# Gate projections of a recurrence in pieces of two to five products between the links of its chain

## The chip, the cores and the metric
The kernel runs on one core of a Trainium2 chip. The metric is the device time of one execution in microseconds (us). All arithmetic is in 32-bit floats. The engines named below are PE (TensorE: its matmuls, and PEld for its weight loads), DVE (VectorE), ACT (ScalarE), POOL (GpSimd) and SP (SyncE, which issues the DMAs).

## The reference, cut to what matters
Two transformer blocks are computed over 256 tokens of width 1024. The second block has two branches from one projection: sparse attention and an RWKV-7 recurrence. Both are gated and merged, and a mixture of 32 experts follows.

```python
xn = _rmsnorm(h, mix_norm_g[l]) * (1.0 + sc1) + sh1
proj = xn @ w_in[l]
q_a, kv_lat, q_i, k_i, w_i, p_shift, gate_a, gate_r = _split(proj, IN_SPLITS)
...
def step(state, inp):
    r_t, d_t, k_t, v_t, kk_t, b_t = inp
    sa = jnp.einsum('bhij,bhj->bhi', state, -kk_t)
    state = state * d_t[:, :, None, :] + sa[..., None] * b_t[:, :, None, :] + v_t[..., None] * k_t[:, :, None, :]
    y = jnp.einsum('bhij,bhj->bhi', state, r_t)
    return state, y
...
merged = jax.nn.sigmoid(gate_a) * (o_attn @ w_branch_attn[l]) + jax.nn.sigmoid(gate_r) * (o_rwkv @ w_branch_rwkv[l])
```

The change touches `gate_a` and `gate_r` (the gate projections: 256 tokens, 1024 in, 2048 out) and the stage in which they are computed, which is the one that turns the token-by-token recurrence into matrices over chunks.

## The kernel before, in words
The recurrence has 8 heads of width 64 and 256 tokens. The stage at L2474 to L2709 makes, for each head and each half of the tokens (16 units `u`), the matrices of the chunked form. This needs the inverse of a triangular 128x128 matrix. It is built by a chain of products in which every link depends on the one ahead of it, over PE, ACT and DVE. Two units, `b` = 0 and 1, go side by side as a **pair**; there are eight pairs, in a loop at L2606. Unit `b` works in the PSUM banks `ps[4b]` to `ps[4b + 3]`.

PE's queue is in the order of the program. In one pair the list `steps` (L2543 to L2592) has twelve steps k = 0 to 11, and of each step the first unit's part comes ahead of the second's:

- k = 0, `start_` (L2514): the six products of both units that everything starts from. It waits for `i_end`, that is for ACT's last copy of the pair ahead (`nmap`, L2636).
- k = 1, 2 and 4, `level` (L2549, products at L2554 and L2556): squarings. Their results are copied by ACT (`sq`, L2620).
- k = 3, 5 and 6, `grow` (L2560): products that DVE adds to the growing inverse (`grown`, L2677). Level 1 waits for DVE's `first` (L2665), seven masked products for each unit.
- k = 7, 8 and 9, `off1`, `off2`, `off3` (L2567 to L2581): a transpose, the products outside the diagonal blocks, and a last grow. `off2` also makes two products into `ps[B + 3][:, 0:128]`, which ACT copies (`uh`, L2627).
- k = 10, `solve` (L2583). DVE copies and spreads its results (`sol`, L2692).
- k = 11, `maps` (L2528): the maps of the state for both units. DVE (L2700) and then ACT (`nmap`) take them out.

The gate projections need 32 tiles of 128x128, each the sum of 8 products over chunks of 128 of the inner dimension (`gate_product`, L2593). 8 tiles are computed in the stage ahead and the other 24 here, three in each pair, `GATE_AFTER = (0, 10, 11)` sets them behind the steps 0, 10 and 11, each as one run of eight products. A product over one chunk is two PE instructions in the trace. Their banks are `gate_bank` (L2496): columns 128 to 255 of ps3, ps3 and ps7. ACT turns each tile into gates (`gate_sigmoid`, L2646) at its places k = 0 and k = 5 of a pair and behind the pair. `side_gate` counts finished tiles, `side_gate_out` the sigmoids. SP loads the weights of the two branch projections when the tenth and the eighteenth tile are done (L2489).

The next stage (L2722) runs the chain of states over the chunks, and behind it come the merge, the router and the experts, whose weights are streamed from memory.

Of the kernel before, what the change touches and what calls it, by code (L numbers as in the profile page):

```python
# [19 lines left out]
P = 128  # L20
# [3 lines left out]
KC = D // P  # L24
# [23 lines left out]
def build(nc, inp, out, debug=None, until=99):  # L48
    ctx = ExitStack()
    with ctx:  # L50
# [5 lines left out]
        def sem(name):  # L56
            if name not in sems:
                sems[name] = nc.alloc_semaphore(name)
            return sems[name]
# [58 lines left out]
        ps = [ctx.enter_context(nc.psum_tensor(f"ps{i}", [P, 512], F32)) for i in range(8)]  # L118
# [1569 lines left out]
        with nc.Block() as block:  # L1688
            @block.sync
            def _(sp):  # L1690
                start_sync(sp)
                attention_sync(sp)
                output_sync(sp)
# [45 lines left out]
        LORA, GATE0 = 6, 7  # L1739
# [44 lines left out]
        def p2_ready(pe, i):  # L1784
            pe.wait_ge(sem(f"p2_loaded{i % MIX_CELLS}"), p2_loads[i])
# [688 lines left out]
        with nc.Block() as block:  # L2474
# [3 lines left out]
            def inst(u):  # L2478


                h, t = 2 * (u // 4) + u % 2, u // 2 % NT
                jo = (h % 2) * 64
                return h, t, slice(jo, jo + 64), h // 2, u % 2
# [7 lines left out]
                        sem(f"branch_loaded{i}"), 16)  # L2491


            GATE_AFTER = (0, 10, 11)

            def gate_bank(i):  # L2496
                return ps[(3, 3, 7)[i % 3]][:, P:2 * P]

            @block.gpsimd
            def _(pool):  # L2500
# [11 lines left out]
            @block.tensor  # L2512
            def _(pe):
                def start_(u):  # L2514

                    if u >= 2:
                        pe.wait_ge(sem("i_end"), u)
                    for i in range(3):
                        for w in (u, u + 1):
                            h, t, js, q, b = inst(w)  # L2520
                            T = slice(t * P, (t + 1) * P)
                            left = (bT_, kT_, aT_)[i]
                            last = pe.matmul(ps[4 * b + i][:, 0:(S, S, P)[i]], ch4(left)[js, q, T],
                                             tl[js, 0:2, q, T] if i < 2 else ch4(bT_)[js, q, T], start=True, stop=True)
                            if i == 2:
                                last.then_inc(sem("i_prod"), 1)

                def maps(u):  # L2528

                    pe.wait_ge(sem("i_gh"), u + 2)  # L2530
                    pe.wait_ge(sem("i_spread"), u + 2)
                    for i in range(3):
                        for w in (u, u + 1):
                            h, t, js, q, b = inst(w)
                            hs = slice(h * 64, (h + 1) * 64)
                            left = (mat(b, UH)[:, 64:P], b_tk[:, t, hs], k_tk[:, t, hs])[i]
                            right = (exp_v[b][:, 0:S], exp_g[b], exp_v[b][:, S:2 * S])[i]
                            last = pe.matmul(ps[4 * b + 2][js, min(i, 1) * S:(min(i, 1) + 1) * S], left, right,
                                             start=(i < 2), stop=(i != 1))
                            if i == 2:  # L2540
                                last.then_inc(sem("i_maps"), 1)

                def steps(u):  # L2543

                    h, t, js, q, b = inst(u)
                    B = 4 * b
                    hs = slice(h * 64, (h + 1) * 64)

                    def level(n, Q, QT, last_level):  # L2549
                        def f():  # L2550
                            pe.wait_ge(sem(f"i_q{b}"), 4 * (u // 2) + n)
                            if n == 1:
                                pe.wait_ge(sem(f"i_pt{b}"), 5 * (u // 2) + 1)
                            last = pe.matmul(ps[B][:, 0:P], mat(b, QT), mat(b, Q), start=True, stop=True)  # L2554
                            if not last_level:
                                last = pe.matmul(ps[B][:, P:S], mat(b, Q), mat(b, QT), start=True, stop=True)  # L2556
                            last.then_inc(sem(f"i_sq{b}"), 1)
                        return f

                    def grow(n, Q, PT):  # L2560
                        def f():
                            pe.wait_ge(sem(f"i_q{b}"), 4 * (u // 2) + n)
                            pe.wait_ge(sem(f"i_pt{b}"), 5 * (u // 2) + n - 1)
                            pe.matmul(ps[B + 1][:, 0:P], mat(b, Q), mat(b, PT), start=True, stop=True).then_inc(sem(f"i_gr{b}"), 1)
                        return f

                    def off1():  # L2567
                        pe.wait_ge(sem(f"i_pt{b}"), 5 * (u // 2) + 4)
                        pe.transpose(ps[B + 2][:, 0:P], mat(b, PTB), ident[:, :]).then_inc(sem(f"i_pd{b}"), 1)

                    def off2():
                        pe.wait_ge(sem(f"i_off{b}"), 2 * (u // 2) + 1)
                        pe.matmul(ps[B + 2][:, P:S], mat(b, OTM), mat(b, QA), start=True, stop=True).then_inc(sem(f"i_xt{b}"), 1)

                        pe.wait_ge(sem("side_gate_out"), 2 + 3 * (u // 2) + (1, 0)[b])
                        pe.matmul(ps[B + 3][:, 0:64], AKT[b], v_tk[:, t, hs], start=True, stop=True)
                        pe.matmul(ps[B + 3][:, 64:128], RKT[b], v_tk[:, t, hs], start=True, stop=True).then_inc(sem(f"i_u{b}"), 1)

                    def off3():
                        pe.wait_ge(sem(f"i_off{b}"), 2 * (u // 2) + 2)  # L2580
                        pe.matmul(ps[B + 1][:, 0:P], mat(b, QB), mat(b, PTB), start=True, stop=True).then_inc(sem(f"i_gr{b}"), 1)  # L2581

                    def solve():  # L2583
                        pe.wait_ge(sem(f"i_pt{b}"), 5 * (u // 2) + 5)
                        pe.wait_ge(sem(f"i_ud{b}"), u // 2 + 1)
                        pe.matmul(ps[B][:, 0:64], mat(b, PTA), mat(b, UH)[:, 0:64], start=True, stop=True)
                        pe.matmul(ps[B][:, 64:P], mat(b, PTA), a_tk[:, t, hs], start=True, stop=True)
                        pe.matmul(ps[B + 1][js, 0:P], a_tk[:, t, hs], mat(b, PTA), start=True, stop=True).then_inc(sem("i_sol"), 1)

                    return [lambda: None if u % 2 else start_(u), level(1, QA, QTA, False), level(2, QB, QTB, False),  # L2590
                            grow(2, QB, PTA), level(3, QA, QTA, True), grow(3, QA, PTB), grow(4, QB, PTA), off1, off2, off3,
                            solve, lambda: maps(u - 1) if u % 2 else None]  # L2592
                def gate_product(i):  # L2593
                    m, t = 4 + i // NT, i % NT
                    if i % 8 == 0:
                        p2_ready(pe, GATE0 + m // 4)
                    if i % 3 == 0 and i:
                        pe.wait_ge(sem("side_gate_out"), 2 + i - 1)
                    if i % 3 == 2:
                        pe.wait_ge(sem("i_ud1"), i // 3 + 1)  # L2600
                    for c in range(KC):
                        last = pe.matmul(gate_bank(i), p2(GATE0 + m // 4)[:, c, (m % 4) * P:(m % 4 + 1) * P],  # L2602
                                         hT[:, c, t * P:(t + 1) * P], start=(c == 0), stop=(c == KC - 1))
                    last.then_inc(sem("side_gate"), 1)

                for pair in range(8):  # L2606
                    for k, (fa, fb) in enumerate(zip(steps(2 * pair), steps(2 * pair + 1))):
                        fa()
                        fb()
                        if k in GATE_AFTER:  # L2610
                            gate_product(3 * pair + GATE_AFTER.index(k))


            @block.scalar
            def _(act):
# [30 lines left out]
                def gate_sigmoid(i):  # L2646
                    m, t = 4 + i // NT, i % NT
                    act.wait_ge(sem("side_gate"), 2 + i + 1)
                    act.activation(gates_sb[:, m // 4, m % 4, t, :], gate_bank(i), ACT.Sigmoid).then_inc(sem("side_gate_out"), 1)

                for pair in range(8):
                    for k, (fa, fb) in enumerate(zip(steps(2 * pair), steps(2 * pair + 1))):
                        if k in (0, 5):
                            gate_sigmoid(3 * pair + k // 5)
                        fa()
                        fb()
                    gate_sigmoid(3 * pair + 2)

            @block.vector
            def _(v):  # L2660
# [341 lines left out]
```

## Time and profile before
| | us |
|---|---|
| median of 3 runs | 1460.09 |
| lowest and highest of them | 1457.9, 1460.11 |
| the profiled execution | 1459.41 |
| its span in the profile | 1457.7 |
| the stage of the change, within the span | 693.2 to 851.6 |

| engine | busy us | share of the span |
|---|---|---|
| PE matmul | 1153.3 | 79% |
| PE weight load | 673.6 | 46% |
| VectorE | 507.6 | 35% |
| ScalarE | 266.2 | 18% |
| GpSimd | 43.2 | 3% |

The shares are averages over stages that have different limits. In a chain like the one of this stage an engine can be busy for most of the time because its instructions overlap with their own waits, so what counts is which wait ends last ahead of each link. The start of a weight load shows when PE takes up a product. The times in the rows below are us from the start of the span.

### The profile page before, as it was taken

The page shows a single profiled execution, that of the slowest core. Times are in us where ns is not written, and L with a number is a line of the kernel's source. Part 1 is how long each engine was busy: PE and PEld are TensorE (multiplying, and loading weights), DVE is VectorE, ACT ScalarE, POOL GpSimd, SP SyncE. Part 2 cuts the span into 40 slices and gives each one's busy share as a digit, 9 for nine tenths or more (in the row PEclk, how much of TensorE's full clock was granted, in tenths as well). Part 3 has the DMA queues.
Part 4 walks back from the last instruction along what each step waited for, and adds up shares of the span by engine and source line. Part 5 has one row for each costly group of instructions (what it writes and reads, how often), then busy time and mean ns, then how long its engine had stood idle before and what let it go on. Part 6 is the DMA issues. An engine that isn't in the chain of part 4 may idle for free. (4 is left out here: it accounts for less than half of the span.)

```text
span 1457.7 us, 17019 instructions
## 1 busy us (share of the span) xinstructions
PE 1153.3 (79%) x6655; PEld 673.6 (46%) x6655; DVE 507.6 (35%) x1284; ACT 266.2 (18%) x666; POOL 43.2 (3%) x111
## 2 busy tenths in 40 slices
PE   5999869999999795799899996959657567666656
PEld 2788444443343483567777775634122221221212
DVE  1569442222222466758444444242101011010111
ACT  2223212211121212235222220012010100101000
POOL 0000000000000200000111100000000000000000
PEclk8999879999999798888999996979877887787888
DMA  9777636999999793111111010755999999999995
GB/s 373 278 278 273 250 124 272 403 428 428 427 428 383 243 362 122 58 63 54 59 59 51 9 59 1 293 231 224 422 421 422 422 421 422 422 422 422 422 421 230
DMA packets 75155, 404.68 MB, mean 278 GB/s; under 512 B 14075, under 2 KB 15288, under 8 KB 41308
## 3 DMA queue, kind: packets, MB, share of 16 engines
q1 hardware_dynamic: 75100, 403.95, 68.7%
q8 instruction: 35, 0.57, 0.2%
q14 instruction: 20, 0.16, 0.0%
HBM read 402.88 MB, written 1.05 MB: 277 GB/s over the span
## 5 line engine op out<-in xcount | busy, mean ns | idle before, releaser
L1151 PE MATMUL ps<-ring,hT_sb 128*32 128x512 f32 x768 | 119.2, 778 | 71.5 <-DMA ring<-in_expert_w_gate 41.5
L1513 PE MATMUL ps<-ring,hT_sb 128*64 128x512 f32 x448 | 113.2, 595 | 4.2 <-DMA ring<-in_expert_w_gate 2.4
L1151 PEld LDWEIGHTS ps<-ring,hT_sb 128*32 128x32 f32 x768 | 29.0, 137 | 154.9 <-issue 94.0
L1151 PE MATMUL ps<-side,hT_sb 128*32 128x512 f32 x256 | 41.5, 808 | 36.1 <-DMA side<-in_expert_w_up 18.1
L607 PE MATMUL ps<-hT_sb,ring 128*128 128x256 f32 x256 | 61.9, 392 | 2.7 <-ACT hT_sb L352 2.7
L1163 PE MATMUL ps<-ring,tmp 128*32 128x512 f32 x384 | 49.2, 659 | 18.5 <-DMA ring<-in_expert_w_down 18.5
L1760 PE MATMUL ps<-hT_sb,ring 128*128 128x256 f32 (+1 forms) x240 | 61.5, 417 | 0.1
L1217 ACT ACTIVATE hT_sb<-ps,modc 128x128 f32<-128x128 f32 x72 | 27.1, 457 | 188.8 <-PE ps L1134 188.8
L1513 PEld LDWEIGHTS ps<-ring,hT_sb 128*64 128x64 f32 x448 | 35.3, 137 | 55.9 <-issue 51.8
L1255 DVE TENSOR_TENSOR tmp<-ps,tmp 128x512 f32<-128x512 f32 x8 | 5.5, 692 | 154.4 <-ACT tmp L1225 154.4
L1521 PE MATMUL ps<-ring,tmp 128*64 128x512 f32 x256 | 56.7, 595 | 0.0
L607 PEld LDWEIGHTS ps<-hT_sb,ring 128*128 128x128 f32 x256 | 47.9, 194 | 13.6 <-issue 4.6
L1266 DVE COPY hT_sb<-ps 128x512 f32<-128x512 f32 x8 | 5.5, 692 | 136.3 <-PE ps L1163 136.3
L1760 PEld LDWEIGHTS ps<-hT_sb,ring 128*128 128x128 f32 (+1 forms) x240 | 47.6, 203 | 10.8 <-issue 3.3
L1584 ACT ACTIVATE hT_sb<-ps,modc 128x128 f32<-128x128 f32 x72 | 27.1, 456 | 126.9 <-PE ps L1503 126.9
L2602 PE MATMUL ps<-hT_sb,ring 128*128 128x128 f32 x384 | 49.2, 281 | 0.0
L2602 PEld LDWEIGHTS ps<-hT_sb,ring 128*128 128x128 f32 x384 | 44.7, 191 | 5.4 <-issue 4.4
L1163 PE MATMUL ps<-side,tmp 128*32 128x512 f32 x128 | 25.4, 967 | 20.5 <-DMA side<-in_expert_w_down 20.5
L1151 PEld LDWEIGHTS ps<-side,hT_sb 128*32 128x32 f32 x256 | 9.7, 143 | 67.8 <-issue 25.3
L1261 DVE TENSOR_TENSOR tmp<-ps,tmp 128x512 f32<-128x512 f32 x8 | 5.5, 691 | 89.0 <-PE ps L1151 89.0
L214 DVE SCALAR_TENSOR_TENSOR acc<-side,cond,acc 128x1024 f32<-128x1024 f32 x28 | 35.8, 1280 | 0.8
L1163 PEld LDWEIGHTS ps<-ring,tmp 128*32 128x32 f32 x384 | 12.1, 120 | 49.3 <-issue 26.2
(515 smaller groups left out, 1906.7 us busy)
## 6 DMA issues: line engine op xcount, KB each, us to landing
ring<-in_expert_w_gate SPq DMA_DIRECT2D x12, 4096.0 KB, 34.5
ring<-in_expert_w_up SPq DMA_DIRECT2D x12, 4096.0 KB, 34.8
ring<-in_expert_w_down SPq DMA_DIRECT2D x12, 4096.0 KB, 33.3
ring<-in_expert_w_down SPq DMA_DIRECT2D x16, 2048.0 KB, 15.9
ring<-in_expert_w_up SPq DMA_DIRECT2D x16, 2048.0 KB, 18.3
ring<-in_expert_w_gate SPq DMA_DIRECT2D x12, 2048.0 KB, 19.4
side<-in_ada_w SPq DMA_DIRECT2D x20, 1024.0 KB, 6.4
ring<-in_w_in SPq DMA_DIRECT2D x9, 2048.0 KB, 8.5
```

Of the source, the lines that this page charges most:

```text
L214: ins = v.scalar_tensor_tensor(a, w, s, a, ALU.mult, ALU.add)
L607: last = pe.matmul(ps[6][:, w * S:(w + 1) * S], cell(2 * w + h // 4)[:, c, (h % 4) * P:(h % 4 + 1) * P], hT[:, c, :], start=(c == 0), stop ...
L1151: last = pe.matmul(bank[es, :], xg[:, c, es], w[:, e, c % 4, :], start=(c == 0), stop=(c == KC - 1))
L1163: last = pe.matmul(out_ps[h][es, :], hidT[:, f, es], w[:, e, f % 2, h * 512:(h + 1) * 512], start=(f == 0), stop=(f == FC - 1))
L1217: last = act.activation(xg[:, c, :], (gate_ps, up_ps)[half][:, (c % 4) * P:(c % 4 + 1) * P], ACT.Identity, scale=modc[:, 2 * KC + c:2 * KC ...
L1255: v.tensor_tensor(hid, gate_ps[:, :], hid, ALU.mult).then_inc(sem("q_silu"), 1)
L1261: v.tensor_tensor(hid, up_ps[:, :], hid, ALU.mult).then_inc(sem("q_hid_done"), 1)
L1513: last = pe.matmul(bank[e * SLOTS:(e + 1) * SLOTS, :], xg[:, c, e * SLOTS:(e + 1) * SLOTS], dst(e, j, par)[:, c, :], start=(c == 0), stop= ...
L1521: last = pe.matmul(out_ps[h][e * SLOTS:(e + 1) * SLOTS, :], hidT[:, f, e * SLOTS:(e + 1) * SLOTS], dst(e, 2, 0)[:, f, h * 512:(h + 1) * 51 ...
L1584: last = act.activation(xg[:, c, :], (gate_ps, up_ps)[half][:, (c % 4) * P:(c % 4 + 1) * P], ACT.Identity, scale=modc[:, 2 * KC + c:2 * KC ...
L1760: last = pe.matmul(ps[SHIFT_BANKS[m]][0:n, 0:S], p2(i)[:, c, o:o + n], hT[:, c, :], start=(c == 0), stop=(c == KC - 1))
L2602: last = pe.matmul(gate_bank(i), p2(GATE0 + m // 4)[:, c, (m % 4) * P:(m % 4 + 1) * P], hT[:, c, t * P:(t + 1) * P], start=(c == 0), stop= ...
```

## The change
The list `GATE_STEPS` takes the place of `GATE_AFTER`. For each of the three tiles of a pair it says behind which step which chunks are multiplied. The first tile: chunks 0 and 1 behind step 0, chunks 2 to 4 behind step 1, chunks 5 to 7 behind step 2. The second: 0 to 2 behind step 3, 3 to 5 behind step 4, 6 and 7 behind step 5. The third: 0 to 2 behind step 9, 3 to 7 behind step 10. Nothing stands behind step 11 any more. The number of products, their shapes and their operands are the same.

The banks are now ps3, ps7 and ps3. The waits follow them: the first tile of a pair waits for the last sigmoid of the pair ahead, the second for ACT's copy of the second unit in the pair ahead (`i_ud1`), the third for that of the first unit in this pair (`i_ud0`). `off2` waits for the sigmoid of the tile that shares its unit's bank. ACT takes the three sigmoids at its places 2, 3 and 5, ahead of the third squaring's copy, ahead of `uh`, and ahead of `nmap`.

```diff
--- before.py
+++ after.py
@@ -2491,10 +2491,10 @@
                         sem(f"branch_loaded{i}"), 16)
 
 
-            GATE_AFTER = (0, 10, 11)
+            GATE_STEPS = ({0: (0, 2), 1: (2, 5), 2: (5, 8)}, {3: (0, 3), 4: (3, 6), 5: (6, 8)}, {9: (0, 3), 10: (3, 8)})
 
             def gate_bank(i):
-                return ps[(3, 3, 7)[i % 3]][:, P:2 * P]
+                return ps[(3, 7, 3)[i % 3]][:, P:2 * P]
 
             @block.gpsimd
             def _(pool):
@@ -2572,7 +2572,7 @@
                         pe.wait_ge(sem(f"i_off{b}"), 2 * (u // 2) + 1)
                         pe.matmul(ps[B + 2][:, P:S], mat(b, OTM), mat(b, QA), start=True, stop=True).then_inc(sem(f"i_xt{b}"), 1)
 
-                        pe.wait_ge(sem("side_gate_out"), 2 + 3 * (u // 2) + (1, 0)[b])
+                        pe.wait_ge(sem("side_gate_out"), 2 + 3 * (u // 2) + (1, 2)[b])
                         pe.matmul(ps[B + 3][:, 0:64], AKT[b], v_tk[:, t, hs], start=True, stop=True)
                         pe.matmul(ps[B + 3][:, 64:128], RKT[b], v_tk[:, t, hs], start=True, stop=True).then_inc(sem(f"i_u{b}"), 1)
 
@@ -2590,25 +2590,31 @@
                     return [lambda: None if u % 2 else start_(u), level(1, QA, QTA, False), level(2, QB, QTB, False),
                             grow(2, QB, PTA), level(3, QA, QTA, True), grow(3, QA, PTB), grow(4, QB, PTA), off1, off2, off3,
                             solve, lambda: maps(u - 1) if u % 2 else None]
-                def gate_product(i):
+                def gate_product(i, first, end):
+
                     m, t = 4 + i // NT, i % NT
-                    if i % 8 == 0:
-                        p2_ready(pe, GATE0 + m // 4)
-                    if i % 3 == 0 and i:
-                        pe.wait_ge(sem("side_gate_out"), 2 + i - 1)
-                    if i % 3 == 2:
-                        pe.wait_ge(sem("i_ud1"), i // 3 + 1)
-                    for c in range(KC):
+                    if first == 0:
+                        if i % 8 == 0:
+                            p2_ready(pe, GATE0 + m // 4)
+                        if i % 3 == 0:
+                            pe.wait_ge(sem("side_gate_out"), 2 + i)
+                        elif i % 3 == 1 and i > 1:
+                            pe.wait_ge(sem("i_ud1"), i // 3)
+                        elif i % 3 == 2:
+                            pe.wait_ge(sem("i_ud0"), i // 3 + 1)
+                    for c in range(first, end):
                         last = pe.matmul(gate_bank(i), p2(GATE0 + m // 4)[:, c, (m % 4) * P:(m % 4 + 1) * P],
                                          hT[:, c, t * P:(t + 1) * P], start=(c == 0), stop=(c == KC - 1))
-                    last.then_inc(sem("side_gate"), 1)
+                    if end == KC:
+                        last.then_inc(sem("side_gate"), 1)
 
                 for pair in range(8):
                     for k, (fa, fb) in enumerate(zip(steps(2 * pair), steps(2 * pair + 1))):
                         fa()
                         fb()
-                        if k in GATE_AFTER:
-                            gate_product(3 * pair + GATE_AFTER.index(k))
+                        for i, part in enumerate(GATE_STEPS):
+                            if k in part:
+                                gate_product(3 * pair + i, *part[k])
 
 
             @block.scalar
@@ -2650,11 +2656,10 @@
 
                 for pair in range(8):
                     for k, (fa, fb) in enumerate(zip(steps(2 * pair), steps(2 * pair + 1))):
-                        if k in (0, 5):
-                            gate_sigmoid(3 * pair + k // 5)
+                        if k in (2, 3, 5):
+                            gate_sigmoid(3 * pair + (2, 3, 5).index(k))
                         fa()
                         fb()
-                    gate_sigmoid(3 * pair + 2)
 
             @block.vector
             def _(v):
```

## Rows read from the trace of the kernel before
**Rows 1.** The chain that ended last, in order of time: start us, us, what.
```profile
1406.63 33.74 DMA side<-in_expert_w_down
```
**Rows 2.** Windows of the stage: us, busy us of engines (instructions), PEclk, DMA share, GB/s.
```profile
733.00:753.00 20.00, 18.45 (x138) 15.31 (x138) 9.14 (x34) 5.08 (x18) 2.83 (x7) 1.00 0.14 39
```
**Rows 3.** Timeline ahead of the stage: start us, us, engine, line, operation, tiles, count.
```profile
672.72 14.37 PEld L2345 LDWEIGHTS ps<-hT_sb,ring 128*128 128x128 f32 x128
```
**Rows 4.** Timeline of the third pair, and the start of the fourth.
```profile
732.80 1.16 PEld L2523 LDWEIGHTS ps<-tmp 64*128 64x128 f32 x12
...
734.08 1.86 PEld L2602 LDWEIGHTS ps<-hT_sb,ring 128*128 128x128 f32 x16
...
735.64 0.28 DVE L2675 TENSOR_TENSOR ring<-ps,pos_t 128x128 f32<-128x128 f32 x1
...
736.03 0.30 PEld L2554 LDWEIGHTS ps<-acc 128*128 128x128 f32 x2
...
737.68 0.30 PEld L2554 LDWEIGHTS ps<-acc 128*128 128x128 f32 x2 [1.12 <-issue]
...
738.12 0.30 PEld L2554 LDWEIGHTS ps<-acc 128*128 128x128 f32 x2
...
738.86 0.30 PEld L2554 LDWEIGHTS ps<-acc 128*128 128x128 f32 x2 [0.22 <-ACT acc L2624]
...
739.30 0.53 PEld L2564 LDWEIGHTS ps<-acc 128*128 128x128 f32 x4
...
739.75 0.59 PEld L2554 LDWEIGHTS ps<-acc 128*128 128x128 f32 x4
...
740.26 0.60 PEld L2564 LDWEIGHTS ps<-acc 128*128 128x128 f32 x4
...
741.27 0.30 PEld L2564 LDWEIGHTS ps<-acc 128*128 128x128 f32 x2 [0.41 <-issue]
...
744.35 0.53 PEld L2581 LDWEIGHTS ps<-acc 128*128 128x128 f32 x4
...
745.23 0.30 PEld L2586 LDWEIGHTS ps<-acc 128*128 128x128 f32 x2 [0.35 <-DVE acc L2680]
...
747.13 1.86 PEld L2602 LDWEIGHTS ps<-hT_sb,ring 128*128 128x128 f32 x16 [0.17 <-issue]
...
747.64 0.41 DVE L2696 TENSOR_TENSOR ring<-acc,gate_t 128x256 f32<-128x256 f32 x1
749.12 0.20 PEld L2538 LDWEIGHTS ps<-side,acc 128*64 128x64 f32 x4
...
750.56 1.86 PEld L2602 LDWEIGHTS ps<-hT_sb,ring 128*128 128x128 f32 x16 [0.39 <-issue]
...
751.17 0.84 ACT L2639 ACTIVATE ring<-ps 64x256 f32<-64x256 f32 x2 [1.67 <-DVE side L2702]
...
752.54 1.16 PEld L2523 LDWEIGHTS ps<-tmp 64*128 64x128 f32 x12
```
**Rows 5.** Timeline, the last gate product of the stage and its sigmoid.
```profile
849.19 2.05 PE L2602 MATMUL ps<-hT_sb,ring 128*128 128x128 f32 x16
...
851.28 0.28 ACT L2649 ACTIVATE ring<-ps 128x128 f32<-128x128 f32 x1 [0.64 <-PE ps L2602]
```
**Rows 6.** PE in windows (PE busy, PEclk), and two groups of its timeline at either clock.
```profile
646.00:648.00 2.00, 1.11 (x8) 0.87 0.00 0
...
872.00:874.00 2.00, 2.00 (x21) 0.69 0.00 0
874.00:876.00 2.00, 2.00 (x6) 0.50 0.00 0
876.00:878.00 2.00, 2.00 (x11) 0.96 0.00 0
...
866.47 1.99 PE L2736 MATMUL ps<-side,ring 128*128 128x256 f32 x8
...
872.59 3.65 PE L2736 MATMUL ps<-side,ring 128*128 128x256 f32 x8
```

## The prediction
> **What bounds the kernel now.** I read the chain that ended last first: the last 440 us are expert weights on the DMA queues, each load released by a product [rows 1], so whatever ends the work ahead of them later moves the end by as much. The recurrence stage, 693.2 to 851.6 us, lies ahead of it and has almost no DMA. There I read the stage windows: the granted clock is 1.00 (2.4 GHz) and PE is busy 18.4 of 20 us [rows 2]. A busy PE says little here, since links of a chain also wait with matmuls in flight, so I went to the timeline of one pair. The eight pairs repeat each other; the one from 732.80 to the next start at 752.54 has a period of 19.74 us [rows 4]. Times below are counted from its start (S = 732.80), by the starts of weight loads, which show when PE takes up a piece.
>
> In it the three gate products of today cost very different amounts [rows 4]:
> - the one behind the start products runs from 1.28 to 3.23. Level 1 of the first half waits for the seventh mask product on VectorE, which ends at 735.92 (3.12), and starts at 3.23. This gate product is free.
> - the one behind the solve runs from 14.33 to 16.32. What it holds up, the maps, needs the VectorE product that ends at 748.05 (15.25), so about 1.0 us of its 1.99 is exposed.
> - the one behind the maps runs from 17.76 to 19.74. The next start needs the ScalarE copy that ends at 752.01 (19.21), so about 0.5 us is exposed.
> So a pair pays some 1.5 us for its gates, 12 us in eight pairs, out of 47 us of gate work. That is all that any placement can win.
>
> **Where PE really waits.** Between 4.88 (level 1, second half) and grow 4, PE runs level 1, level 2, grow 2, level 3, grow 3 nearly without a gap: 4.88, 5.32, 6.06 (after 0.22 us of idleness), 6.50, 6.95, 7.46 [rows 4]. The larger gaps are the 1.12 us ahead of 4.88, which lies between the two halves of one step, where no piece is put, and 0.41 us ahead of 8.47. This stretch, where 14 of the 24 products go, is already bound by PE.
>
> **The price of a product.** 128 instructions of the same shape back to back have loads over 14.37 us, 0.112 each [rows 3]; a product over one chunk is two of them, 0.224 us. Three are 0.67, two 0.45, eight 1.79; the whole gate behind the solve takes 1.99 until the maps start, 0.20 more, which I give to the change of tile shape.
>
> **The change step by step** (before in brackets, all from [rows 4]):
> 1. Behind the start products two products instead of eight. PE is then idle from 1.73 to 3.23. Level 1 still waits for VectorE: nothing is won, 1.5 us of free cover is given up.
> 2. Behind level 1 (ends 5.32) three products: level 2 of the first half at 5.99 [5.32], second half at 6.43 [6.06, which is when its copy from ScalarE came, so it no longer waits], end 6.88. Three more: grow 2 at 7.55 [6.50].
> 3. Grow 2 takes 0.45, three products: level 3 at 8.67 [6.95]; 0.45 and three more: grow 3 at 9.79 [7.46]; 0.45 and two: PE free at 10.69. Grow 4 came 1.01 behind grow 3, 0.41 of it idle, waiting for VectorE's sum of grow 3's result; that gives 10.80 [8.47]. These last two products are hidden. So of 3.13 us inserted (14 products) 2.33 is on the chain at grow 4, and 0.80 is hidden.
> 4. The transposes and the off-diagonal products keep their distances, 3.08 us to off 3: 13.88 [11.55]. Off 3 takes 0.53, three products 0.67; solve at 15.08, where it came 0.88 behind off 3 [12.43]. Shift 2.65.
> 5. Solve takes 1.90, to 16.98. Five products and the same 0.20: maps at 18.30 [16.32]. VectorE would let them start 2.82 behind solve, at 17.90, so 0.4 us of the old exposure stays. Shift 1.98.
> 6. No gate behind the maps: the next start comes when ScalarE's copy is done, 2.89 behind the maps, and about 0.06 for the semaphore: 21.25 [19.74].
> So a period is 1.51 us longer. In the last pair what follows the maps is the end of the stage: today the last gate's sigmoid ends at 851.56 [rows 5], then it is the copy, which by the same distances (the gate at 849.19, the maps 1.44 ahead of it, the copy's end 2.89 behind them) ends at 850.64, 0.92 us earlier. That pair is 1.98 - 0.92 = 1.06 longer. Sum: 7 x 1.51 + 1.06 = **+11.6 us**. If the 0.20 is not paid by a piece of five and the second halves, which are shifted some 0.15 less at grow 4, decide, it is 1.2 a pair: +9. If each of the eight pieces pays as much as 0.05 (the wait ahead of grow 3 shows 0.06 over four instructions), +0.3 a pair: +14.
>
> **Waits and queues.** ScalarE now takes the first gate's sigmoid ahead of the third squaring copy, the second ahead of the copies of the off-diagonal step, the third ahead of the state map. Each takes 0.28 [rows 5] and each gate is complete at least 1 us before the copy behind it is released (first gate 7.55, level 3's copy 9.2; second 10.69, the off-diagonal copies over 13; third 18.1, the map 20.3), so I cost them at nothing; if one of them were late, it would be 0.28 a pair, 2 us. On PE the new waits of the gates are for copies of the previous pair, or of this pair's first half at off 2, done a whole step earlier. The banks are swapped so that the second gate lies beside the second half's work; off 2 waits for sigmoids that are then long done. SyncE's two branch loads wait for the tenth and the eighteenth gate, and shift by a few us, far ahead of their use. GpSimd's spreads are released by the maps and are done in 3 us of a 20 us period. No DMA moves otherwise.
>
> **The clock.** What the new order does besides is leave PE lean. From the end of the start products (1.28) to level 1 of the second half (4.88) it has 8 instructions of 128 columns in 3.6 us; today there are 20. No stretch of the stage is as lean now, and the clock holds. In the stage ahead, where PE had 8 short instructions in the 2 us from 646, the clock fell to 0.50 (1.2 GHz) [rows 6]. What a fall costs: eight instructions of 256 columns take 1.99 us at the full level and 3.65 at the half one, and the granted clock of the stretches around the latter (0.69, 0.50 and 0.96 over 2 us each) makes some 3.4 us at the half level [rows 6], so 3.4 x (1 - 1.99/3.65) = 1.6 us, all of it on the chain, since behind level 1 PE has no gap left up to grow 4. How many pairs fall the trace doesn't show: bounds none and eight. I take two, nearer to none, because dense work stands on both sides of the lean stretch: +3.2 us (an estimate).
>
> The Trainium skill, TensorE: Matmul & The Clock Gate, section "A second HAM failure mode: psum-queue depth-cycling", says that a PE that idles briefly between groups of matmuls, cycling through banks, has its clock swing between the two levels. By it all eight pairs could fall, which would be the third case below; the trace of before has such short idles in each pair and the clock stays at 1.00, so I give it a small chance.
>
> **Forecast.** The profiled execution took 1459.4 us (its span is 1457.7, 1.7 lies around it); the median of the runs is 0.7 above it. 1459.4 + 11.6 + 3.2 = 1474.2, and with the 0.7 **1474.9 us** for the median.
>
> **Cases.**
> - A, the forecast: the pieces are exposed, and the clock falls in some pairs (one to four): 1471 to 1479. Chance 0.48. For it: the packed stretch and the lean one.
> - B: exposed, and the clock stays: 1460.1 + 11.6 = 1471.7 (1469 to 1474 by the bounds). Chance 0.30. For it: granted 1.00 in all eight pairs today.
> - C: exposed, and the clock falls in five to eight: up to 1460.1 + 11.6 + 12.8 = 1484.5. Chance 0.08.
> - D, the other side: the pieces are hidden. Place: between level 1 and grow 4. The links there are pairs of halves, and each waits for a copy on ScalarE (0.75 to start) or a sum on VectorE; if those waits, not PE, set the pace, the 3.13 us vanish in them. The net of a pair is the shift at grow 4 less 0.82 (0.32 added at solve, 0.67 won to the maps, 0.47 to the start), so it decides at a shift of 0.8, where I find 2.33. With a shift of nothing it is -0.8 a pair, about 7 us, 1453. Against it: the loads of five steps follow each other within 0.06 us but for one gap of 0.22. Chance 0.06.
> - E: the change does nothing to be seen, with the shift near 0.8 (half of the pieces hidden by waits that the starts of loads don't show): 1457 to 1463. Chance 0.08, of which 0.07 is within 0.2% (2.9 us, about what a measurement of this kernel can tell from no change).
> Slower by over 0.2%: A, B, C and the rest of E, 0.87. Faster: D, 0.06. Within: 0.07. The range 1465 to 1483 holds A and B with their bounds and most of C, and leaves out D, E and the top of C, some 0.16.
>
> **What would show it.** In the trace of after: an idle PE of some 1.5 us ahead of level 1 (1.73 to 3.23) in each pair; level 2 starting 1.1 us behind level 1's second half instead of 0.44; grow 4 at 10.8; a period near 21.2 where the clock is 1.00; no PE work between the end of the maps and the next start; in some pairs a granted clock of 0.50 behind the lean stretch. I am wrong if grow 4 comes by 9.3, which makes it D or E; if the period is 21.2 but the stages behind take the difference back; or if the clock is at 1.00 throughout, which makes it B.

## The result and the profile after
The changed kernel takes 1475.5 us (median of 4 runs, 1474.6 to 1477.1), the kernel before 1459.8 (4 runs). The ratio is 1.0115, with a 95% interval of 1.0101 to 1.0129: slower, by 15.7 us. The profiled execution took 1477.1 us, the highest of the four, with a span of 1475.4.

The page of after: busy time of PE, its granted clock in 40 slices, and the end of the chain that ended last.

```profile
PE 1150.9 (78%) x6655; PEld 677.0 (46%) x6655; DVE 507.6 (34%) x1284; ACT 266.1 (18%) x666; POOL 43.2 (3%) x111
...
PEclk8999869999999797889999997888887887887888
...
DMA 25%; PE 6%; DVE 0%; issue 0%; ACT 0%; DVEq 0%; SPq 0%; ACTq 0%
```

PE runs the same 6655 matmul instructions. The end is what it was in [rows 1], expert weights on the DMA queues, only later. The page has nothing that names the change; the stage has.

The eight pairs of after in windows, from one start to the next (the last to the first product of the next stage). Columns: us, PE busy us (instructions), PEclk, DMA share, GB/s.

```profile
693.70:716.59 22.89, 18.86 (x135) 0.93 0.27 92
716.59:737.72 21.13, 17.22 (x134) 1.00 0.00 1
737.72:760.50 22.78, 18.96 (x134) 0.93 0.25 93
760.50:781.63 21.13, 17.22 (x134) 1.00 0.00 1
781.63:802.76 21.13, 17.22 (x134) 1.00 0.00 1
802.76:825.53 22.77, 18.85 (x135) 0.93 0.26 93
825.53:846.66 21.13, 17.22 (x134) 1.00 0.00 1
846.66:868.46 21.80, 17.22 (x134) 1.00 0.01 1
```

A period at full clock is 21.13 us where it was 19.74 [rows 4]. Three pairs have a mean clock of 0.93 and take about 1.65 us more. Before, all eight had 1.00 [rows 2]. The stage, from its first start product to the first product of the next stage, is 174.8 us; it was 159.1 (693.23 to 852.28). The difference is 15.7 us, the whole of what the medians show. The span of the profiled execution is 17.7 us longer: 0.5 of it lies ahead of the stage (which starts at 693.70 and not 693.23), 15.7 in it, and 1.5 behind it, where the next stage took 62.6 us against 59.1 and all that follows it 544.4 against 546.3. The next stage has falls of the clock of its own in both kernels (mean 0.79 before and 0.73 after), and it takes anything from 58.9 to 62.6 us in the profiles of all the runs below, so this difference is not put down to the change.

The fourth pair of after, weight loads only, at full clock. It starts at 760.50; L2606 is now the gate product.

```profile
760.50 1.16 PEld L2523 LDWEIGHTS ps<-tmp 64*128 64x128 f32 x12 [1.89 <-ACT ring L2645]
761.79 0.52 PEld L2606 LDWEIGHTS ps<-hT_sb,ring 128*128 128x128 f32 x4
763.73 0.30 PEld L2554 LDWEIGHTS ps<-acc 128*128 128x128 f32 x2 [1.43 <-issue]
...
765.37 0.30 PEld L2554 LDWEIGHTS ps<-acc 128*128 128x128 f32 x2 [1.12 <-issue]
...
765.81 0.75 PEld L2606 LDWEIGHTS ps<-hT_sb,ring 128*128 128x128 f32 x6
766.48 0.30 PEld L2554 LDWEIGHTS ps<-acc 128*128 128x128 f32 x2
...
768.05 0.53 PEld L2564 LDWEIGHTS ps<-acc 128*128 128x128 f32 x4
768.49 0.75 PEld L2606 LDWEIGHTS ps<-hT_sb,ring 128*128 128x128 f32 x6
769.16 0.53 PEld L2554 LDWEIGHTS ps<-acc 128*128 128x128 f32 x4
...
770.28 0.53 PEld L2564 LDWEIGHTS ps<-acc 128*128 128x128 f32 x4
770.73 0.53 PEld L2606 LDWEIGHTS ps<-hT_sb,ring 128*128 128x128 f32 x4
771.29 0.62 PEld L2564 LDWEIGHTS ps<-acc 128*128 128x128 f32 x4
...
774.35 0.53 PEld L2581 LDWEIGHTS ps<-acc 128*128 128x128 f32 x4
774.79 0.75 PEld L2606 LDWEIGHTS ps<-hT_sb,ring 128*128 128x128 f32 x6
775.47 0.30 PEld L2586 LDWEIGHTS ps<-acc 128*128 128x128 f32 x2
...
777.37 1.19 PEld L2606 LDWEIGHTS ps<-hT_sb,ring 128*128 128x128 f32 x10 [0.17 <-issue]
778.68 0.20 PEld L2538 LDWEIGHTS ps<-side,acc 128*64 128x64 f32 x4
```

Three things to see. PE idles 1.43 us ahead of level 1 (763.73), where the first tile used to be, and again 1.89 ahead of the start products, where the third was. Between 765.37 and 771.29 no row has a bracket, that is, no idle time ahead of it: all pieces but the last lengthen the path, and the last fills the 0.41 us of idleness that stood ahead of grow 4 [rows 4]. And level 1 itself comes no earlier, 3.23 us behind the start as before.

The wait tables of the two kernels fit this, from the side of those who wait for PE. Before, from 693 to 873 us (us in total, times, longest):

```profile
DVE acc L2680 <- PE ps L2564: 24.6, 25, 2.3
...
ACT acc L2624 <- PE ps L2556: 15.7, 24, 1.3
```

After, the same two waits under their new line numbers, of the same stretch:

```profile
ACT acc L2630 <- PE ps L2556: 50.9, 27, 4.0
DVE acc L2685 <- PE ps L2564: 48.1, 25, 5.0
```

ScalarE's wait for a squaring and VectorE's wait for a grow have grown by 35.2 and 23.5 us. They overlap, so they don't add up to the loss, and a part of ScalarE's is only moved: its wait for the gate products fell from 41.4 to 21.6 us, since the sigmoids stand in other places. What the pieces cost is read from the starts above.

### The profile page after: what moved, and what is told of

The parts are those of the page before. It is cut to its first block and busy times, and to the rows that moved or that the text cites. A ratio compares the mean times of both kernels' runs of the same rounds, so it can differ in the third digit from the quotient of the medians.

```text
span 1475.4 us, 17021 instructions
## 1 busy us (share of the span) xinstructions
PE 1150.9 (78%) x6655; PEld 677.0 (46%) x6655; DVE 507.6 (34%) x1284; ACT 266.1 (18%) x666; POOL 43.2 (3%) x111
## 5 line engine op out<-in xcount | busy, mean ns | idle before, releaser
L2606 PE MATMUL ps<-hT_sb,ring 128*128 128x128 f32 x384 | 57.4, 288 | 0.0
L607 PEld LDWEIGHTS ps<-hT_sb,ring 128*128 128x128 f32 x256 | 48.1, 195 | 13.8 <-issue 4.6
L2606 PEld LDWEIGHTS ps<-hT_sb,ring 128*128 128x128 f32 x384 | 50.4, 200 | 2.3 <-issue 1.4
L2685 DVE TENSOR_TENSOR acc<-ps,acc 128x128 f32<-128x128 f32 x64 | 18.7, 292 | 52.3 <-PE ps L2564 48.1
```

The source lines that it names most:

```text
L607: last = pe.matmul(ps[6][:, w * S:(w + 1) * S], cell(2 * w + h // 4)[:, c, (h % 4) * P:(h % 4 + 1) * P], hT[:, c, :], start=(c == 0), stop ...
L2685: v.tensor_tensor(mat(b, dst), ps[B + 1][:, 0:P], mat(b, src), ALU.add).then_inc(sem(f"i_pt{b}"), 1)
```

## The experiments
**Theory 1**, that of the prediction: between level 1 and grow 4 PE itself is the bound, so that products set there are paid; where PE waits, they are free; and the emptied stretches are lean enough (a few instructions between idle times) for the clock to fall. **Theory 2**: the loss is in what came with the pieces, the swapped banks, the new waits and the sigmoids ahead of ScalarE's copies. For the clock the rival is that its falls are not tied to the lean stretches.

Both kernels and all nine runs in one table. The period is that of pairs at full clock, from start to start; "at half" counts pairs in which the clock fell; the stage is measured as above; all three come from one profiled execution of each kernel; the ratio is to the kernel before on the same chip.

| kernel | period | at half | stage | median us | ratio, 95% interval |
|---|---|---|---|---|---|
| before | 19.73 | 0 | 159.1 | 1459.8 | |
| after | 21.13 | 3 | 174.8 | 1475.5 | 1.0115 (1.0101 to 1.0129) |
| first tile whole again | 20.09 | 0 | 161.5 | 1461.8 | 1.0023 (1.0007 to 1.0040) |
| first tile alone in pieces | 20.74 | 2 | 170.4 | 1470.7 | 1.0087 (1.0067 to 1.0108) |
| second tile alone in pieces | 19.99 | 2 | 164.3 | 1465.5 | 1.0056 (1.0037 to 1.0075) |
| the same, gap behind the solve filled | 19.98 | 0 | 161.1 | 1461.9 | 1.0024 (1.0013 to 1.0034) |
| after, gap ahead of level 1 filled | 21.13 | 0 | 169.9 | 1472.0 | 1.0097 (1.0080 to 1.0114) |
| before, four more behind step 3 | 20.54 | 0 | 165.6 | 1467.7 | 1.0063 (1.0047 to 1.0078) |
| before, two more behind step 5 | 19.72 | 0 | 159.0 | 1458.3 | 1.0001 (0.9990 to 1.0011) |
| all where PE waits | 18.26 | 0 | 147.2 | 1446.9 | 0.9924 (0.9910 to 0.9937) |
| the same, none between the halves | 18.86 | 0 | 152.0 | 1451.0 | 0.9947 (0.9932 to 0.9962) |

### One part undone: the first tile whole
```diff
-            GATE_STEPS = ({0: (0, 2), 1: (2, 5), 2: (5, 8)}, {3: (0, 3), 4: (3, 6), 5: (6, 8)}, {9: (0, 3), 10: (3, 8)})
+            GATE_STEPS = ({0: (0, 8)}, {3: (0, 3), 4: (3, 6), 5: (6, 8)}, {9: (0, 3), 10: (3, 8)})
```


> The order of after, but the first tile of each pair again as one run of eight products behind the start products; banks, waits and sigmoids stay those of after. Theory 1 (PE is packed between level 1 and grow 4, and the stretch ahead is lean): only the 6 products that went into the packed stretch come back, so grow 4 comes 1.3 us earlier, a period is 20.1 us, the granted clock is 1.00 in all eight pairs, and the time is 2 to 3 us above before, 1462. Theory 2 (the loss is in the swapped banks, the new waits or the sigmoids ahead of ScalarE's copies): these are all still there, so most of the 15.7 us stays, 1472 to 1475.

Measured: 1461.8, period 20.09, no fall. The one line takes back 13.3 of the 15.7 us of the stage, with banks, waits and sigmoids as in after. So theory 2 can't be the main loss: all that is left for it, together with the pieces of the second and third tile, is 2.4 us.

### One part alone: the first tile in pieces
```diff
-            GATE_AFTER = (0, 10, 11)
+            GATE_STEPS = ({0: (0, 2), 1: (2, 5), 2: (5, 8)}, {10: (0, 8)}, {11: (0, 8)})
...
-                        if k in (0, 5):
-                            gate_sigmoid(3 * pair + k // 5)
+                        if k in (2, 5):
+                            gate_sigmoid(3 * pair + (2, 5).index(k))
```


> The kernel before with its banks and waits; only its first tile is in pieces of 2, 3 and 3 products behind steps 0, 1 and 2, with its sigmoid ahead of the third squaring's copy. Theory 1: six products move from free cover into the packed stretch, at most 1.3 us a pair and about 1.0 by the chain, a period of 20.7 to 21.0 at full clock, and one or more pairs fall to half clock (the stretch behind the start products is as lean as in after), 1.6 us each: 1466 to 1471. Theory 2: without the banks and waits of after the time stays near before, 1460 to 1462.

Measured: 1470.7, period 20.74, falls in the first and the sixth pair. The first tile costs 1.01 us a pair on the kernel before and 1.04 within after (21.13 less 20.09), and it brings the falls with it.

### One part alone: the second tile in pieces
```diff
-            GATE_STEPS = ({0: (0, 2), 1: (2, 5), 2: (5, 8)}, {3: (0, 3), 4: (3, 6), 5: (6, 8)}, {9: (0, 3), 10: (3, 8)})
+            GATE_STEPS = ({0: (0, 8)}, {3: (0, 3), 4: (3, 6), 5: (6, 8)}, {11: (0, 8)})
...
-                        if k in (2, 3, 5):
-                            gate_sigmoid(3 * pair + (2, 3, 5).index(k))
+                        if k in (2, 3):
+                            gate_sigmoid(3 * pair + (2, 3).index(k))
                         fa()
                         fb()
+                    gate_sigmoid(3 * pair + 2)
```


> The order of after for the second tile alone (3, 3 and 2 products behind steps 3, 4 and 5); the first tile is whole behind the start products and the third whole behind the maps. Theory 1: 6 products (1.3 us) go on the chain, 1.0 us exposed behind the solve is won back: period 20.1, 2 to 3 us above before, 1462; if the clock falls, in the gap of 1 us behind the solve that is now empty, 1.6 us more each time. Theory 2 expects nothing here but the cost of the banks, like the first run: over 1470.

Measured: 1465.5 with two falls, and a period of 19.99 at full clock, 0.26 over before. With the first tile whole the third tile in pieces costs 0.10 more (20.09 less 19.99). So a period's 1.40 us divide into 1.04 for the first tile, 0.26 for the second and 0.10 for the third. The 0.26 is net of what the empty place behind the solve wins back, and it would hold any cost of the banks, waits and sigmoids, which are those of after in this run; no run separates these.

The falls sit in another place than those of after. Weight loads of this run around the first of them:

```profile
746.45 0.19 PEld L2588 LDWEIGHTS ps<-acc,side 128*64 128x64 f32 x2
747.79 0.29 PEld L2538 LDWEIGHTS ps<-side,acc 128*64 128x64 f32 x4 [1.15 <-DVE ring L2702]
...
748.70 0.24 PEld L2538 LDWEIGHTS ps<-ring,side 128*64 128x64 f32 x2 [0.19 <-issue]
```

Nothing stands behind the solve here, PE idles 1.15 us, and the maps then run at half clock: their loads are 0.24 us for two, with pauses, and the maps take 2.76 us to the next group (747.79 to 750.55) where they took 1.44 [rows 4].

### That gap filled
Three products of 128x128 are added behind the solve in each pair, into the third tile's bank; nothing uses their results.
```diff
+                def fill(i, n):
+                    pe.wait_ge(sem("i_ud0"), i // 3 + 1)
+                    for c in range(n):
+                        pe.matmul(gate_bank(i), hT[:, c, 0:P], hT[:, c, P:2 * P], start=True, stop=True)
...
+                        if k == 10:
+                            fill(3 * pair + 2, 3)
```


> The run with the second tile alone in pieces, and three idle products behind the solve, where that run's PE stands idle for 0.9 us ahead of the maps and where the clock fell in two pairs just as the maps began (747.8 and 809.2 us). Clock theory: that gap is its second lean place; filled, the clock stays at 1.00, all periods are 20.0 to 20.1, and the kernel is 3 us faster than without the fill, 1462. Rival: the falls come with the time of the execution and not with the gap, and stay: 1465.

Measured: 1461.9. The interval of its ratio lies below that of the run without the fill and just clear of it (1.0034 against 1.0037). The granted clock in the whole stage, first without, then with the fill:

```profile
691.12:855.40 164.28, 144.83 (x1073) 0.98 0.11 39
```
```profile
690.49:851.60 161.11, 148.62 (x1121) 1.00 0.11 40
```
24 products more, which are 48 instructions (1121 against 1073), and the stage is 3.2 us shorter.

### The same in after: the lean stretch filled
Six such products behind the first tile's two, into the second tile's bank.
```diff
+                def fill(i, n):
+                    m = 4 + i // NT
+                    if i > 1:
+                        pe.wait_ge(sem("i_ud1"), i // 3)
+                    for c in range(n):
+                        pe.matmul(gate_bank(i), hT[:, c, 0:P], hT[:, c, P:2 * P], start=True, stop=True)
...
+                        if k == 0:
+                            fill(3 * pair + 1, 6)
```


> The kernel after with six idle products of 128x128 (their results are overwritten) behind the two of the first tile, where PE stands idle for 1.5 us: 48 products more in all, 10.8 us of PE work more. Clock theory: the lean stretch is what lets the clock fall, so it is 1.00 in all eight pairs, every period is 21.1, the three falls of 1.64 us go, and the kernel is 4 to 5 us faster than after with more work: 1470.5. Rival: the falls have nothing to do with that stretch, and they stay (1475), or the products cost their time (1475 and more, period over 22).

Its third pair, weight loads (start at 734.79), and the whole stage in one window:

```profile
736.07 0.52 PEld L2606 LDWEIGHTS ps<-hT_sb,ring 128*128 128x128 f32 x4
736.51 1.42 PEld L2616 LDWEIGHTS ps<-hT_sb 128*128 128x128 f32 x12
738.02 0.30 PEld L2554 LDWEIGHTS ps<-acc 128*128 128x128 f32 x2
```
```profile
692.39:862.27 169.88, 148.09 (x1168) 1.00 0.11 38
```
The twelve added instructions (L2616) take the idle time, level 1 (738.02) comes 3.23 us behind the start as ever, the clock is 1.00 in all eight pairs, and all periods are 21.1. The stage is 4.9 us shorter than in after: the three falls are gone and nothing else is. The median is 3.5 us lower, 1472.0. But the two kernels were measured on different occasions and the intervals of their ratios overlap (from 1.0101 to 1.0114), so that the whole kernel became faster is not shown here; what shows the cause is the clock and the length of the stage. In the pair of runs ahead the ratios show it too.

### The price of a product, in two places
On the kernel before, products of 128x128 with unused results go into ps7: four behind step 3, or two behind step 5.
```diff
+                def fill(i, n):
+                    if i > 2:
+                        pe.wait_ge(sem("side_gate_out"), 2 + i)
+                    for c in range(n):
+                        pe.matmul(ps[7][:, P:2 * P], hT[:, c, 0:P], hT[:, c, P:2 * P], start=True, stop=True)
...
+                        if k == 3:
+                            fill(3 * pair, 4)
```
The other has `if k == 5` and 2 in the last two lines.

> The kernel before with four idle products of 128x128 (0.90 us of PE) behind step 3 in each pair, results unused. Theory 1 (packed): nearly all is on the chain, 0.8 us a pair, period 20.5, 6 to 7 us above before: 1466. Rival (hidden by the waits for ScalarE and VectorE): period 19.7 to 19.9, within 2 us of before.

> The kernel before with two idle products (0.45 us) behind step 5, where grow 4 waits for VectorE, results unused. Theory 1: hidden, period 19.75 and the time within 1 us of before, 1460. Rival (any product between links is paid): 0.45 us a pair, period 20.2, 1463.5.

Measured: four behind step 3 cost 0.81 of their 0.90 us in every period, 6.5 us in the stage (the median is 9.4 above that of before; in its profile the stage also starts 2.0 us later, at 695.2, after work that is the same. That start is anywhere from 690.5 to 695.5 in the profiles of these runs, and is not of the change). Two behind step 5 cost nothing: 19.72, ratio 1.0001. Whether a product is paid is decided by the place and not by being between two links.

### All products where PE waits
In this version tiles run over the end of a pair. In each pair: behind step 0 eight products, between the first and the second half of level 1 four, behind step 5 two, behind step 9 one, behind the solve three, behind the maps six.
```diff
+            GATE_STEPS = {0: ((0, 2, 8), (1, 0, 2)), 5: ((1, 6, 8),), 9: ((2, 0, 1),), 10: ((2, 1, 4),), 11: ((2, 4, 8), (3, 0, 2))}
+            GATE_MID = (1, 2, 6)
...
+                return ps[(7, 3, 3)[i % 3]][:, P:2 * P]
...
                         fa()
+                        if MID and k == 1:
+                            gate_product(3 * pair + GATE_MID[0], *GATE_MID[1:])
                         fb()
```
Each entry is a tile counted from the pair's first, and the chunks from and to. The first tile waits for `i_ud1`, the second for the sigmoids of all tiles up to the last but one, the third for `i_ud0`; the sigmoids are at ScalarE's places 0 and 3 and behind the pair, and `off2` again waits for those of the tiles in its unit's bank.

> All 24 products of a pair where PE waits in the trace: eight behind the start products, four between the two halves of level 1, two behind step 5, one behind step 9, three behind the solve, six behind the maps; tiles run over the end of a pair, banks ps7, ps3, ps3. Theory 1: nothing is exposed but a tenth or two; period 18.4, clock 1.00, the stage 11 us shorter: 1449. Rival (the two halves of a step lose when anything stands between them, since the second half waits behind it): the four in the middle are paid, period 19.2, 1455.

Weight loads of its fourth pair, which starts at 749.38 (L2609 is the gate product here), and the fifth, from 767.64, as a window:

```profile
750.66 1.86 PEld L2609 LDWEIGHTS ps<-hT_sb,ring 128*128 128x128 f32 x16
752.61 0.30 PEld L2557 LDWEIGHTS ps<-acc 128*128 128x128 f32 x2
...
753.05 0.97 PEld L2609 LDWEIGHTS ps<-hT_sb,ring 128*128 128x128 f32 x8
754.25 0.30 PEld L2557 LDWEIGHTS ps<-acc 128*128 128x128 f32 x2 [0.22 <-issue]
...
763.68 0.74 PEld L2609 LDWEIGHTS ps<-hT_sb,ring 128*128 128x128 f32 x6 [0.17 <-issue]
764.66 0.20 PEld L2541 LDWEIGHTS ps<-side,acc 128*64 128x64 f32 x4 [0.23 <-DVE ring L2711]
...
766.11 1.42 PEld L2609 LDWEIGHTS ps<-hT_sb,ring 128*128 128x128 f32 x12 [0.38 <-issue]
767.64 1.17 PEld L2526 LDWEIGHTS ps<-tmp 64*128 64x128 f32 x12
```
```profile
767.64:785.90 18.26, 17.88 (x135) 1.00 0.00 1
```
The second half of level 1 comes 4.87 us behind the start, when it always came, with four products in what was a gap of 1.12. The maps come 0.98 us behind the first load of the gate products that follow the solve, instead of 1.99 [rows 4]. 18.26 is 1.47 less than 19.73, which is the 1.5 us that the prediction found to be all a pair pays for its gates. The stage is 11.9 us shorter, the median 1446.9: faster than both kernels.

> As the run ahead, but the four products stand behind both halves of level 1 and not between them. Theory 1: 0.6 us of their 0.9 are exposed, period 18.9 to 19.0, 5 us above the run ahead: 1454. Rival: no difference between the two.

```diff
-            MID = True
+            MID = False
```
Measured: 1451.0, period 18.86. Behind both halves the same four products cost 0.60 us a pair, 4.8 us in the stage.

## Why the prediction was right
It gave 1474.9; measured were 1475.5. By its own steps, times from a pair's start, the pair at 760.50:

1. Two products behind the start, PE idle, level 1 at 3.23: at 3.23, with 1.43 idle.
2. Level 2 at 5.99, grow 2 at 7.55: 5.98 and 7.55.
3. Level 3 at 8.67, grow 3 at 9.79, grow 4 at 10.80: 8.66, 9.78, 10.79. The last two products are hidden; the run with two more behind step 5 shows the same by itself.
4. Off 3 at 13.88, solve at 15.08: 13.85 and 14.97. This is the one term of the period that was mis-sized. I let off 3 take 0.53, which is how long its loads are in the row; to the next load it is 0.44 (774.35 to 774.79).
5. Maps at 18.30: 18.18, the same 0.1 carried on. The 0.20 was there: ten loads from 777.37 to 778.68 take 1.31, five times 0.224 is 1.12. That it is the change of tile shape was assumed, and no run isolates it.
6. Next start at 21.25: 21.13. 1.40 us a period, not 1.51.

The clock was case A as it was put: three pairs fell, two were taken. Each fall cost 1.64 us (22.78 and 22.77 against 21.13) where 1.6 was worked out from two groups in another stage (3.4 x (1 - 1.99/3.65) is in truth 1.55). One of them, in the pair from 737.72; level 2's loads after the piece are 0.43 apart, where they are 0.22 apart at 766.48:

```profile
743.03 1.03 PEld L2606 LDWEIGHTS ps<-hT_sb,ring 128*128 128x128 f32 x6
743.94 0.55 PEld L2554 LDWEIGHTS ps<-acc 128*128 128x128 f32 x2
744.37 0.55 PEld L2556 LDWEIGHTS ps<-acc 128*128 128x128 f32 x2
```

The sum made again with measured terms: seven periods at 1.40 are 9.8, the last pair 0.96 (21.80 against 20.84), three falls 4.9: 15.7. The prediction had 0.9 us too much for the periods and the last pair and 1.7 too little for the clock, which leaves it 0.9 short; and it started from a median of 1460.1 where the one measured with after is 1459.8. So the miss of 0.6 is small by luck: its parts cancel. The mechanism of the 10.8 us is not luck, since every start was worked out ahead.

The rivals: D and E needed a shift at grow 4 of 0.8 or less; it is 2.32. B would have been 21.1 in all eight pairs. That it is the lean stretches behind which the clock falls was an inference from windows of another stage; the two fills show it, and so does the table: the three orders with such a stretch have 7 falls in 24 pairs, the eight without have none in 64. In the second tile's run the lean stretch lay behind an empty solve. The prediction did not name it, the expectation of that run did; in after the third tile's five products stand there.

How many pairs fall was a guess and stays one. The eight pairs of after are alike on PE and three fell; with the first tile alone it was the first and the sixth, with the second alone the third and the sixth.

The windows of after show something that these pairs have in common: all three have a DMA share of 0.25 to 0.27, and the five others at most 0.01. Are the transfers the cause? Finer windows of the pair from 737.72 say no, the fall is over before its transfer starts (the pair from 802.76 has the same order):

```profile
742.00:744.00 2.00, 1.38 (x10) 0.86 0.00 0
744.00:746.00 2.00, 2.00 (x11) 0.50 0.00 0
746.00:748.00 2.00, 2.00 (x16) 0.79 0.00 0
...
750.00:752.00 2.00, 1.84 (x10) 1.00 0.21 45
```

Pairs with such a transfer also keep the clock at 1.00 in the kernel before and in after with the gap filled. What decides which of the lean pairs fall, the runs don't show.

The Trainium skill's warning about short idles between groups (TensorE: Matmul & The Clock Gate, section "A second HAM failure mode: psum-queue depth-cycling"), which I had weighed as case C, is half borne out. The clock did swing, in 3 of 8 pairs, with 1.4 and 1.1 us of idleness on either side of a short level 1. Idles and banks in turn are not enough by themselves: in the last two versions tiles cycle through banks as well, and the clock is 1.00 in the whole stage. Nor does the longest single idle decide: the 1.89 us ahead of the start products stand also in the run with the first tile whole and in after with the gap filled, and there no pair falls.

## What to carry to other kernels
Filler work in a dependent chain goes where the engine in question waits. The starts of its instructions in one period show these places to a tenth of a microsecond: a large busy share hides them, and so does the idea that "between links" means "free". Look inside the steps too: the best gap of this chain lay between two halves of one step. Before moving filler out of a gap, ask what the gap will do when it is empty; here that cost 4.9 us in clock on top of 10.8 in the schedule.

## What the hardware did that I had not expected
- Work that nobody uses made a stage faster: 48 products more in after's lean stretch took 4.9 us off it (174.8 to 169.9), and 24 more in the second tile's run 3.2 us (164.3 to 161.1), because the granted clock stayed at 2.4 GHz. For the second the ratios of the whole kernel show it as well (1.0056 and 1.0024).
- A lean stretch in a single pair is enough to lose the clock, and the loss is small and of one size: a fall in the stage holds the half level for about 3.4 us (worked out from the windows of 742 to 748: 0.56, 2.0 and 0.84) and costs 1.5 to 1.65 us, in three different orders of the work.
- The schedule is exact enough to be worked out. The ten starts listed above, computed from another kernel's trace, came out within 0.12 us each.
